# Masking the stick-breaking scores by products, a plain sigmoid, and another order of the convolution steps

## The reference

```
def stick_breaking_attention(q, k, v):            # 4 heads of 64, blocks of 128 queries
    z = einsum('bhqd,bhkd->bhqk', qb, kp) * scale
    mask = arange(t1)[None, :] < arange(t0, t1)[:, None]
    log_skip = where(mask, log_sigmoid(-z), 0.0)
    later = cumsum(log_skip, axis=3, reverse=True) - log_skip
    att = where(mask, exp(log_sigmoid(z) + later), 0.0)
    outs.append(einsum('bhqk,bhkd->bhqd', att, vp))

def token_mix(h, ...):
    gdn_qkv = silu(causal_dwconv(gdn_qkv, gdn_conv_w))       # 4 taps
    g_q, g_k = l2_normalize(g_q) * 128 ** -0.5, l2_normalize(g_k)
    beta = sigmoid(gdn_b)
    log_decay = -exp(gdn_a_log) * softplus(gdn_a + gdn_dt_bias)
    o_gdn = gated_delta_rule_chunked(g_q, g_k, g_v, log_decay, beta)
    ...
```

## Time and profile before

| | us |
|---|---|
| median of three runs | 1630.29 |
| lowest, highest | 1628.84, 1633.93 |
| the profiled execution: time | 1633.93 |
| the profiled execution: span | 1632.1 |
| PE busy | 1606.6 (98%) |
| POOL busy | 1235.0 (76%) |
| ACT busy | 887.7 (54%) |
| DVE busy | 777.0 (48%) |
| DMA, mean rate | 158 GB/s |

### The profile page before, as it was taken

How to read it: one execution, slowest core, us unless ns; L and a number is a source line. 1 busy time by engine, 2 the same in 40 slices (tenths; PEclk the granted TensorE clock), 3 DMA queues, 4 the chain that set the end, 5 groups by cost and what they waited for, 6 DMA issues and landing times.

```text
span 1632.1 us, 32133 instructions
## 1 busy us (share of the span) xinstructions
PE 1606.6 (98%) x12958; PEld 1558.5 (95%) x12958; DVE 777.0 (48%) x1484; ACT 887.7 (54%) x1217; POOL 1235.0 (76%) x964
## 2 busy tenths in 40 slices
PE   9999999999999999999999999999999999999997
PEld 8999999999999999999999999999998899988996
DVE  3221286657321276221477656221476755666555
ACT  5334485348344386344684266334587565666653
POOL 7988867237988869888767158989687667886674
PEclk9999999999999999999989999999999999999998
DMA  7555543214555545555434124555445333543341
GB/s 291 210 189 194 182 147 136 80 53 145 210 188 182 186 143 194 184 186 193 164 130 144 38 104 163 204 193 189 157 155 181 130 129 132 182 182 137 124 149 56
DMA packets 36848, 258.57 MB, mean 158 GB/s; under 512 B 4080, under 2 KB 4336, under 8 KB 6000
## 3 DMA queue, kind: packets, MB, share of 16 engines
q1 hardware_dynamic: 35712, 254.59, 43.6%
q10 hardware_dynamic: 1008, 2.09, 0.4%
HBM read 255.61 MB, written 1.05 MB: 157 GB/s over the span
## 4 chain that ended last, share of the span: by engine, by line
PE 92%; ACT 4%; DVE 3%; issue 1%; DMA 1%; SPq 0%; POOL 0%; ACTq 0%; DVEq 0%
PE psum L774 23%; PE psum L776 23%; PE psum L775 23%; PE psum L912 5%; PE psum L762 3%; PE psum L757 3%; PE psum L758 3%; PE psum L1291 1%; ACT wh L1425 1%; PE psum L1302 1%; DMA raw<-wstream 1%; PE psum L1319 1%; PE psum L924 0%; PE psum L1285 0%; PE psum L954 0%
## 5 line engine op out<-in xcount | busy, mean ns | idle before, releaser
L1390 POOL TENSOR_TENSOR wl<-raw,wh 128x512 fp32r<-128x512 f32 x960 | 1234.8, 1321 | 375.0 <-ACT wh L1425 366.2
L774 PE MATMUL psum<-xs,wh 128*128 128x256 f32 x1984 | 571.0, 288 | 1.5 <-issue 1.5
L776 PE MATMUL psum<-xs,wl 128*128 128x256 f32 x1984 | 561.9, 283 | 0.0
L775 PE MATMUL psum<-xs,wh 128*128 128x256 f32 x1984 | 559.4, 282 | 0.0
L1425 ACT ACTIVATE wh<-raw 128x2048 fp32r<-128x2048 f32 x237 | 453.3, 1914 | 112.5 <-PE psum L776 90.9
L774 PEld LDWEIGHTS psum<-xs,wh 128*128 128x128 f32 x1984 | 380.1, 192 | 6.2 <-issue 4.9
L775 PEld LDWEIGHTS psum<-xs,wh 128*128 128x128 f32 x1984 | 377.5, 190 | 0.8 <-issue 0.5
L776 PEld LDWEIGHTS psum<-xs,wl 128*128 128x128 f32 x1984 | 377.6, 190 | 0.0
L774 PE MATMUL psum<-arena_r,wh 128*128 128x256 f32 x1168 | 331.5, 284 | 0.0
L775 PE MATMUL psum<-arena_r,wh 128*128 128x256 f32 x1168 | 329.3, 282 | 0.0
L776 PE MATMUL psum<-arena_r,wl 128*128 128x256 f32 x1168 | 329.2, 282 | 0.0
(11 more groups left out here) (328 smaller groups left out, 1892.3 us busy)
## 6 DMA issues: line engine op xcount, KB each, us to landing
raw<-wstream SPq DMA_DIRECT2D x239, 1024.0 KB, 4.8
cst<-consts SPq DMA_DIRECT2D x1, 1824.0 KB, 15.3
raw<-wstream SPq DMA_DIRECT2D x4, 256.0 KB, 6.3
out<-xT SPq DMA_DIRECT2D x4, 256.0 KB, 2.3
sm<-small ACTq DMA_DIRECT2D x2, 359.5 KB, 7.5
xT<-xt ACTq DMA_DIRECT2D x2, 256.0 KB, 5.0
xT<-xt ACTq DMA_DIRECT2D x1, 512.0 KB, 7.7
sm<-small ACTq DMA_DIRECT2D x2, 147.0 KB, 4.9
```

What stands on the lines that cost most here:

```text
L774: mm(o, a[0], b[0], start=start, stop=False, skip_group_check=shared)
L775: mm(o, a[0], b[1], start=False, stop=False, skip_group_check=shared)
L776: return mm(o, a[1], b[0], start=False, stop=stop, skip_group_check=shared)
L1390: return nc.gpsimd.tensor_tensor(wl[:, s, quarter(q)], raw[:, s, quarter(q)], wh[:, s, quarter(q)].bitcast(F32), ALU.subtract)
```

## The change

Four things are done at once, all inside the token mix of the two layers.

1. **Mask by products.** `capped` only scales. `skips` has one more instruction, which multiplies s2 by -1 and by a mask of ones and zeros into s1, and `later` sums s1 in place of s2; `argument` adds the sum instead of subtracting it. After `exp_of` a new DVE step `masked` multiplies the weights in s2 by the mask, and `pv` waits for its signal `sbm_`. `masked(0)` and `masked(1)` stand behind `level_a(2)`, `masked(2)` and `masked(3)` behind the decay of q. The constant tile `sbm` is now 0 and 1.
2. **Sigmoid instead of tanh.** beta is ACT's own Sigmoid instead of 0.5 tanh(x/2) + 0.5, and the DVE instruction that completed the latter is gone. The Sigmoid comes last and carries the signal `g_t2` that the Ln carried.
3. **ACT's order.** ACT now waits for the log decay and spreads it (`gbc`) ahead of `conv_in(2)`; `conv_out` goes 0, 1, 4, 5, 2, 3 with `conv_in(3)` behind `conv_out(1)`, and the copy of weights `feed("qkv", 3)` stands ahead of `conv_out(2)` and `conv_out(3)`.
4. **DVE's order.** `conv2(5)` stands ahead of the two instructions that make the log decay, not behind them.

```
-                link(A(tiny[:, 56:64], tiny[:, 8:16], ACT.Tanh, scale=0.5))
                 sync()
-                A(tiny[:, 32:40], tiny[:, 32:40], ACT.Ln, bias=1.0).then_inc(*g_t2.tick(0))
+                link(A(tiny[:, 32:40], tiny[:, 32:40], ACT.Ln, bias=1.0))
+                sync()
+                A(tiny[:, 56:64], tiny[:, 8:16], ACT.Sigmoid).then_inc(*g_t2.tick(0))
                 nc.scalar.preload_act_table(ACT.Silu)
-                conv_in(2)
                 wait(g_rd, 0)
                 A(gbc, along(tiny[:, 16:24], P), ACT.Copy).then_inc(*g_bc.tick(0))
+                conv_in(2)
                 feed("qkv", 2)
                 conv_out(0)
+                conv_out(1)
                 conv_in(3)
-                conv_out(1)
+                conv_out(4)
+                conv_out(5)
+                feed("qkv", 3)
                 conv_out(2)
                 conv_out(3)
-                feed("qkv", 3)
-                conv_out(4)
-                conv_out(5)
...
                 conv2(1)
                 conv2(4)
+                conv2(5)
                 wait(g_t2, 0)
...
-                link(TS(tiny[:, 56:64], tiny[:, 56:64], 0.5, 0.5, ALU.mult, ALU.add))
-                conv2(5)
                 conv2(2)
...
-                    link(STT(s0, bank1("sbz", h)[:, 0:3 * P], SBD ** -0.5, K("sbm"), ALU.mult, ALU.add))
+                    link(TS(s0, bank1("sbz", h)[:, 0:3 * P], SBD ** -0.5, None, ALU.mult))
...
-                    TTo(s2, s2, s1, ALU.add).then_inc(*sbk_.tick(h))
-                    wait(sbk_, h)
+                    link(TTo(s2, s2, s1, ALU.add))
+                    sync()
+                    STT(s1, s2, -1.0, K("sbm"), ALU.mult, ALU.mult).then_inc(*sbk_.tick(h))
                     link(TTo(s0, s0, s2, ALU.subtract))
...
+                def masked(h):
+                    wait(sbe_, h)
+                    s2 = sbs[:, h % 2, 2, :]
+                    TTo(s2, s2, K("sbm"), ALU.mult).then_inc(*sbm_.tick(h))
```

More of the change, by code:

```diff
@@ L503, in hybrid @@
         cvd = sig("conv_done", [2 * m + t for m in CONV_ORDER for t in range(2)])
-        css = sig("conv_silued", range(len(CONV_ORDER)))
+        css = sig("conv_silued", CONV_ORDER)
         sqd = sig("qk_squared", range(4))
@@ L546, in hybrid @@
         sba_ = sig("sb_argument_ready", range(4))
-        sbe_ = sig("sb_attention_ready", range(4))
+        sbe_ = sig("sb_exp_ready", range(4))
+        sbm_ = sig("sb_attention_ready", range(4))
         mxs = sig("mixed_sb_ready", [0, 1])
@@ L987, in later @@
                     pe.wait_ge(*sbk_.at(li, h))
-                    ls = sbs[:, h % 2, 2, :]
+                    ls = sbs[:, h % 2, 1, :]
                     mm(o[:, 0:P], K("after"), ls[:, 0:P], start=True, stop=True)
@@ L999, in pv @@
                     for h in (2 * m_, 2 * m_ + 1):
-                        pe.wait_ge(*sbe_.at(li, h))
+                        pe.wait_ge(*sbm_.at(li, h))
                         r = SBD * (h % 2)
@@ L2276, in argument @@
                     s0 = sbs[:, h % 2, 0, :]
-                    TTo(s0, s0, bank1("later", h)[:, 0:3 * P], ALU.subtract).then_inc(*sba_.tick(h))
+                    TTo(s0, s0, bank1("later", h)[:, 0:3 * P], ALU.add).then_inc(*sba_.tick(h))
+                def masked(h):
+                    wait(sbe_, h)
+                    s2 = sbs[:, h % 2, 2, :]
+                    TTo(s2, s2, K("sbm"), ALU.mult).then_inc(*sbm_.tick(h))
                 capped(0)
@@ L2318, in layer1 @@
                 level_a(2)
+                masked(0)
+                masked(1)
                 tap(0)
@@ L2337, in layer1 @@
                     TTo(q, q, er[:, tt, :, :], ALU.mult).then_inc(*qdd.tick(tt))
+                masked(2)
+                masked(3)
                 tap(2)
@@ L2674, in constants @@
         put("lev", lev(s), at=n * P)
-    put("sbm", np.where(np.concatenate([i < j, np.ones((P, P), bool), i < j], axis=1), 0.0, -1e9))
+    put("sbm", np.concatenate([i < j, np.ones((P, P), bool), i < j], axis=1))
     half = MR // 2
```

## The result

| | before | changed |
|---|---|---|
| median, us | 1630.24 | 1644.51 |
| lowest, highest | 1628.84, 1633.93 | 1641.01, 1645.9 |
| profiled execution: span | 1632.1 | 1642.7 |
| profiled execution: time | 1633.93 | 1644.49 |

(The median of before is here over four executions, the three from ahead of the forecast and one more.) The change makes the kernel slower: ratio 1.0081, interval [1.0058, 1.0103]. The forecast was 1637.7 us, with a range of 1632.5 to 1643. The direction was right and the size was not: the time moved by 14.3 us instead of 7.4, and the range missed it.

A forecast was written before the change was run, and what follows sets the result against it. TensorE's own stream was taken to set the time, so edits could only add waits: 2.8 at ssq, 0.8 at the sixth level and 3.8 at pv 1, 7.4 us over the median of 1630.29, giving 1637.7; range 1632.5 to 1643.

The forecast's parts named there:

- The bound: Whole kernel: TensorE, busy 98% of the span, sets the time; edits gain only from waits that hardly exist.
- ACT's chain: Log decay and convolutions: gbc starts at 235.6, ACT runs without a gap, last square ends at 247.7; extra table load costs nothing.
- Rival E: ACT's table switches cost double, adding 5.2 us for 12.6 in all, 1642.9 us; chance 0.02.
- The wait at ssq: TensorE waits for ACT's last square, 1.6 us in the first layer and 1.2 in the second, 2.8 together.
- The clock: Nothing in the sum; a fall behind pv 1 might come in each layer, up to 3.2 us more.
- Rival D: Later narrow stretches let the clock stay up, each fall avoided giving back 1.6 us; two give 1634.5, four 1631.3; chance 0.12.
- Rival B: The three new waits, plus a clock fall behind pv 1 once or twice: 1639.3 to 1640.9 us; chance 0.2.
- The masks: New DVE mask instructions: 0.4 us wait at the sixth level and 1.9 at pv 1, in each of two layers.
- Rival C: Smaller waits, through masked at 0.47 us (1634.7) or ACT ahead at ssq (1634.9); chance 0.17.
- Against the median: The 7.4 us added to the median of 1630.29, giving 1637.7; the profiled execution, 1633.93, would make 1641.3.

The follow-up runs named there:

- e_sig: Kernel before with only the Sigmoid in place of tanh (one table load more), both orders as before: 1628.82 us, ratio 1.0002.
- after2: The changed kernel run once more, for a second trace: 1641.97 us, ratio to before 1.0087.
- e_feed: Changed kernel with ACT's copy feed(z, 0) ahead of exp_of(2), so POOL's work runs earlier: 1643.83 us, ratio to before 1.0089.
- e_front: Kernel before with Sigmoid and the new ACT and DVE orders, mask as before: 1635.77 us, ratio 1.0041.
- e_order: Kernel before with only the new ACT and DVE orders, Tanh kept: 1636.02 us, ratio 1.0046.
- e_early: Changed kernel with masked(2) and masked(3) ahead of the decay of q: 1640.62 us, ratio to before 1.0073.
- e_mask: Kernel before with only the mask by products: 1634.95 us, ratio 1.0035.
- e_slot: Changed kernel with the copy feed(qkv, 3) back behind conv_out(2) and conv_out(3): 1638.37 us, ratio to before 1.0053.
- e_old_early: Kernel before with mask by products and Sigmoid, old orders, masked(2) and masked(3) ahead of the decay of q: 1634.25 us, ratio 1.0028.
- e_best: Kernel before with product masks and Sigmoid, old orders, early feed(z, 0), last subtraction of skips(2) and skips(3) behind level_x(4): 1629.56 us, ratio 1.0006.
- e_mix: Kernel before with the 32 narrow matmuls of ssq spread in fours among tiles of sbq and sbk: 1624.03 us, ratio 0.998.
- e_fill: Changed kernel with 7 dense matmuls, results unused, ahead of TensorE's wait at ssq: 1637.46 us, ratio to before 1.005.
- e_front_fill: Kernel before with Sigmoid, new ACT and DVE orders, and 7 unused dense matmuls ahead of the ssq wait: 1634.77 us, ratio 1.0035.

## Why the forecast of the waits held and that of the time did not

**The bound.** Right: TensorE's stream sets the time, nothing was gained, and every new wait is on the path. The profiled spans differ by 10.6 us, the new waits of that trace (3.0 twice, 0.3 twice, 1.2 + 0.8 twice) add up to 10.6, and both traces have 37.4 us of low clock ahead of the kernel's last stretch. That this pair agrees so well is luck in one respect: before's profiled execution was its slowest.

**ACT's chain.** Right, row by row. This is ACT of the changed kernel, against the earlier trace rows:

```profile
232.61 0.21 ACT L1606 ACTIVATE tiny<-tiny 128x8 f32<-128x8 f32 x1
232.84 1.28 ACT L1607 ACT_TABLE_LOAD   x1
...
235.61 1.06 ACT L1610 ACTIVATE arena<-tiny 128x1024 f32<-128x1024 f32 x1 [1.49 <-DVE tiny L2193]
...
243.22 1.91 ACT L1426 ACTIVATE wh<-raw 128x2048 fp32r<-128x2048 f32 x1
...
246.85 0.63 ACT L1585 ACTIVATE arena<-arena 128x512 f32<-128x512 f32 x1
```

The Sigmoid ends at 232.8 as worked out, `gbc` starts at 235.61 (forecast 235.6) after ACT waited 1.49 for DVE, the second slot starts at 243.22 (243.4), and the last square ends at 247.48 (247.7). Rival E fell with these rows: a load takes 1.28 us, here as in the earlier trace rows, where the next instruction starts 0.02 behind it. The Trainium skill (ScalarE: Activation LUTs, What ACT_TABLE_LOAD costs) has 2.66 us for a switch, a drain included; the trace has half of it, and `e_sig`, the edit with the load, has ratio 1.0002.

**The wait at ssq.** The releasing end was right, the waiting end was not. I took TensorE's arrival, 246.17 and 843.50, from an execution in which the clock had fallen ahead of it in both layers, and did not see that a fall there hides a part of the wait. Without it the waits are 3.0 and 3.0; with it, in `after2`, 1.4 and 1.4. The mean over executions is between: the rest grew by 7.7 to 9.1 in all. So this term was low by 0.3 to 1.7 us, not enough to explain the miss.

**The clock.** This is the step that failed: the forecast put the clock at nothing, and it cost 5.5 to 6.3 us. I had the price of a low stretch right (it costs half its length) and gave it a chance of 0.2 behind `pv 1`. I did not ask the same of the wait at `ssq`, though it stands directly in front of 32 matmuls with a single column, where before's clock fell already for 3.4 us. Idle time and the narrow block now lie together, and in the traces with the whole wait (the changed kernel and `e_feed`) the clock is low there for 10.2 us in each layer, in those with about half of it (`after2`, `e_front`, `e_order`) for 6.8; `e_early`, with 1.1 and 1.4 us of wait, has 3.4 and 10.2. `e_mask` has all the waits of `pv 1` and loses 0.9 us to the clock; `e_order` and `e_front` have the wait at `ssq` alone and lose 3.2 to 4.8; `e_slot` shortens that wait and loses 1.6. Rival D (fewer falls) looked at the same stretches and had the sign wrong. But before's 3.4 is no fixed measure, and the falls at `ab` come and go as well. `e_mask`, without any wait at `ssq`, has 6.8 in its second layer:

```profile
844.60:851.20 6.60, 6.60 (x32) 6.60 (x33) 0.60 (x3) 4.39 (x5) 2.30 (x3) 0.50 0.42 159
```

So count the low clock at `ab` and at `ssq` of both layers together, in each profiled execution. In the six traces with a wait of 0.9 us or more at `ssq` and no filler (the changed kernel, `after2`, `e_front`, `e_order`, `e_early`, `e_feed`) it is 20.4 to 27.2 us, 22.1 in the mean. In the six without that wait (before, `e_mask`, `e_sig`, `e_slot`, `e_old_early`, `e_best`) it is 13.6 to 17.0, 15.9 in the mean; with the filler 13.6 and 17.0, and with the sums spread (`e_mix`) 6.8. Elsewhere ahead of the last stretch the two groups are alike, 14.7 and 15.3. Half of the difference is 3.1 us, so the traces place about half of the 5.5 to 6.3 us at `ab` and `ssq`. The rest they do not place: it may be noise, and `e_old_early` (+3.2, uncertain by about 1.3, with no wait at `ssq`) hints that something else can cost clock too.

What stays open is how idle time and narrow matmuls share in it: `e_fill` takes away idle time and not the block, `e_mix` the block, and each lowers the clock's part, but `e_front_fill` did so only weakly.

Rival B, a fall behind `pv 1`, came once, in the second layer of the changed kernel's first trace, and in none of the other nine layers with these waits (both of `after2`, `e_mask`, `e_slot` and `e_fill`, and the first layer of this trace):

```profile
950.40:953.60 3.20, 3.20 (x16) 3.05 (x15) 0.72 (x2) 1.53 (x3) 0.00 (x0) 0.50 0.87 323
```

**The masks.** Nearly right. Forecast 0.4 for `p1` of the sixth level, measured 0.3 in each layer. Forecast 1.9 at `pv 1`, measured 1.23 + 0.77 = 2.0 and 1.27 + 0.77. The reason was right as well. Here are the decay, the masks and the tap on DVE, then POOL:

```profile
342.87 3.38 DVE L2346 TENSOR_TENSOR arena<-arena 128x512 f32<-128x512 f32 x2
...
346.17 3.16 DVE L2284 TENSOR_TENSOR arena<-arena,cst 128x384 f32<-128x384 f32 x2
...
349.25 0.87 DVE L2319 SCALAR_TENSOR_TENSOR arena<-arena,sm 128x256 f32<-128x256 f32 x2
...
342.75 6.16 POOL L1391 TENSOR_TENSOR wl<-raw,wh 128x512 fp32r<-128x512 f32 x4 [35.51 <-ACT wh L1426]
```

A mask takes 1.6 us (forecast 1.4 to 1.5). POOL is through at 348.91, so the tap, which took 2.91 in the earlier trace rows, now takes 0.87: the masks took the tap's place beside POOL, and what they pay the tap saves. `e_feed` is the proof by displacement: no POOL, two masks in 1.02 us, as those of heads 0 and 1 have in the changed kernel. Rival C, cheap masks, is out. The Trainium skill (SBUF — State Buffer, Who interferes with whom) says that a VectorE instruction with two SBUF inputs contends with a GpSimd instruction that reads SBUF. This trace agrees: a mask reads two SBUF tiles and took 1.6 us beside POOL, against 0.51 without.

**Against the median.** The sum was added to the median of 1630.29, though it was made from an execution with both falls ahead of `ssq`, 3.6 us slower. For the waits alone that does no harm (1630.2 + 7.7 to 9.1 = 1638 to 1639); it hides that the same falls are part of the answer.

## What to carry to other kernels

When a change makes the busiest engine wait, cost the wait and then ask what stands behind it: the low clock cost more here (5.5 to 6.3 us, about half of it placed at `ab` and `ssq`) than the forecast erred on all waits (0.3 to 1.7). When a wait is worked out as one engine's end less another's arrival, check the granted clock ahead of the arrival, and work it out for an execution without the fall too. To hide a block of narrow matmuls, spread it among dense ones: the only edit of this study that gained clear of the noise.

## What the runs showed of the hardware beyond that

- The same 32 narrow matmuls, cut into eight groups of four and spread over 6.5 us, lost no clock in the trace of `e_mix`: nothing at 0.50 from 243 to 256 us, nor at that place in the second layer. The kernel's time fell by 0.2%.
- Ahead of the kernel's last stretch the low clock lasted 3.4, 6.8 or 10.2 us in these traces, at the same few places of the program, and not in each execution: the fall behind `ab` was there in `after2` and not in the first profile of the same kernel.
- Beside POOL's subtractions (four in 5.9 to 6.2 us), a DVE instruction with both inputs in SBUF took 1.5 to 1.6 us for 384 elements and 0.51 to 0.56 alone. Moving POOL's work picked which instruction pays; `e_best` lost nothing by it because TensorE did not wait long for those that paid: there the mask product of `skips(3)` took 1.51 us, and the last subtraction of `skips(2)`, at 1.68, stood behind `level_x`.
